# Down projection of a two-block model on one core: seven block products for 7 of 22 k pairs, and channel units in alternating pass order

## What is computed

```python
h = rmsnorm(x, g_ffn[l])                       # 256 x 2048
u = causal_dwconv(h @ w_up[l], ffn_conv_w[l]) + ffn_conv_b[l]
gate, val = jnp.split(u, 2, axis=-1)           # 256 x 5632 each
x = x + (jax.nn.silu(gate) * val) @ w_down[l]  # the down projection: 5632 x 2048 weights
...
return rmsnorm(x, g_final)
```

## Time and profile before

| | us |
|---|---|
| median of 3 runs | 1964.65 |
| lowest, highest | 1964.58, 1966.03 |
| the profiled execution | 1964.4 |
| its span, first to last instruction | 1962.6 |
| TensorE busy in it | 1944.7 (99%) |
| VectorE busy | 1289.4 (66%) |
| ScalarE busy | 1028.8 (52%) |
| granted TensorE clock | 0.999 of full |
| the down projection's matmuls | from 1713.8 to 1952.9, 239.1 |

### The profile page before, as it was taken

How to read it: one execution, slowest core, us unless ns; L and a number is a source line. 1 busy time by engine, 2 the same in 40 slices (tenths; PEclk the granted TensorE clock), 3 DMA queues, 4 the chain that set the end, 5 groups by cost and what they waited for, 6 DMA issues and landing times.

```text
span 1962.6 us, 28709 instructions
## 1 busy us (share of the span) xinstructions
PE 1944.7 (99%) x9868; PEld 1645.5 (84%) x9868; DVE 1289.4 (66%) x1806; ACT 1028.8 (52%) x1503; POOL 47.1 (2%) x74
## 2 busy tenths in 40 slices
PE   8999999999999999999999999999999999999998
PEld 7788888888888888888888888888888888888886
DVE  6655675656655676655768765778778787754444
ACT  5533576664433576654544444555555555544443
POOL 1000030000000020000100000000000000000000
PEclk9999999999999999999999999999999999999999
DMA  8666445545566545545666445556555565565553
GB/s 297 202 194 192 143 157 154 160 151 186 182 195 193 147 161 172 155 155 181 209 193 190 154 168 186 181 183 192 184 190 190 184 192 184 191 214 193 194 193 139
DMA packets 246726, 357.29 MB, mean 182 GB/s; under 512 B 15303, under 2 KB 136481, under 8 KB 246109
## 3 DMA queue, kind: packets, MB, share of 16 engines
q1 hardware_dynamic: 245004, 349.35, 55.8%
q0 software_dynamic: 1616, 6.61, 1.0%
HBM read 352.75 MB, written 3.16 MB: 181 GB/s over the span
## 4 chain that ended last, share of the span: by engine, by line
PE 96%; DVE 1%; ACT 1%; issue 1%; DMA 1%; SPq 0%; DVEq 0%; ACTq 0%
PE acc L368 21%; PE acc L345 19%; PE acc L347 19%; PE acc L346 19%; PE acc L361 11%; PE aux L425 2%; PE aux L833 1%; DVE sb_w_lo L308 1%; PE aux L851 1%; PE aux L850 1%; PE aux L814 1%; DMA sb_stage<-w_kv 0%; PE aux L820 0%; PE aux L822 0%; PE aux L821 0%
## 5 line engine op out<-in xcount | busy, mean ns | idle before, releaser
L308 DVE TENSOR_TENSOR sb_w_lo<-sb_stage,sb_w_hi 128x1024 fp32r<-128x1024 f32 x652 | 799.4, 1228 | 513.8 <-ACT sb_w_hi L303 506.9
L303 ACT ACTIVATE sb_w_hi<-sb_stage 128x1024 fp32r<-128x1024 f32 x652 | 688.7, 1059 | 640.4 <-PE acc L347 372.0
L368 PE MATMUL acc<-sb_xT,sb_w_hi 128*128 128x512 f32 x1856 | 455.3, 392 | 0.0
L368 PEld LDWEIGHTS acc<-sb_xT,sb_w_hi 128*128 128x128 f32 x1856 | 337.6, 189 | 62.6
L345 PE MATMUL acc<-sb_w_hi,sb_xT 128*128 128x512 f32 x768 | 306.6, 399 | 0.4 <-issue 0.4
L347 PE MATMUL acc<-sb_w_hi,sb_xT 128*128 128x512 f32 x768 | 299.8, 390 | 0.0
L346 PE MATMUL acc<-sb_w_lo,sb_xT 128*128 128x512 f32 x768 | 299.6, 390 | 0.0
L361 PEld LDWEIGHTS acc<-sb_xT,sb_w_lo 128*128 128x128 f32 x1856 | 245.6, 191 | 13.3
L361 PE MATMUL acc<-sb_xT,sb_w_lo 128*128 128x256 f32 x1856 | 252.3, 284 | 0.0
L345 PE MATMUL acc<-sb_w_hi,sb_mT 128*128 128x512 f32 x560 | 224.9, 402 | 1.6 <-issue 1.0
L347 PE MATMUL acc<-sb_w_hi,sb_mT 128*128 128x512 f32 x560 | 218.8, 391 | 0.0
(11 more groups left out here) (255 smaller groups left out, 1472.0 us busy)
## 6 DMA issues: line engine op xcount, KB each, us to landing
sb_stage<-w_in SPq DMA_DIRECT2D x248, 512.0 KB, 3.9
sb_stage<-w_up SPq DMA_DIRECT2D x176, 512.0 KB, 3.4
sb_stage<-w_out SPq DMA_DIRECT2D x96, 512.0 KB, 3.5
sb_stage<-w_down SPq DMA_DIRECT2D x88, 512.0 KB, 4.3
sb_stage<-w_kv SPq DMA_DIRECT2D x16, 512.0 KB, 6.8
sb_stage<-w_ukv SPq DMA_DIRECT2D x16, 512.0 KB, 3.4
sb_stage<-w_uq SPq DMA_DIRECT2D x12, 512.0 KB, 3.5
sb_kz<-mem SPq DMA_DIRECT2D x8, 256.0 KB, 7.2
```

The costliest lines, as they stand in the source:

```text
L303: act.activation(w_hi[:, j % RING, 0:size], stage[:, j % RING, 0:size], ACT.Copy).then_inc(hi_ready, 1)
L308: dve.tensor_tensor(w_lo[:, j % RING, 0:size], stage[:, j % RING, 0:size], w_hi[:, j % RING, 0:size].bitcast(F32), ALU.subtract).then_inc( ...
L368: mm = pe.matmul(acc[:, 2 * pair + c, :], hi[:, k, c * P:(c + 1) * P], both, start=first and k == 0, stop=last and k == 3)
```

## The change

It has two parts.

**Pass order.** In `product_cols` the unit at k tile 0 and the one at k tile 8 take the main passes first, the other two the rest passes first. Before, only the one at k tile 0 did. The table is a row of the TensorE program: one group of four units in the first turn of the feed-forward loop, before and then after (`sb_w_hi` is a main pass, `sb_w_lo` a rest pass).

The core of the diff:

```diff
+SEVEN = 7
+DOWN_PAIRS = [[[7, 8], 0, [9, 10], 1, [11, 12], 2, [13, 14], 3, [15, 16], 4, [17, 18], 5, [19], 6, [20, 21]],
+              [[7, 8], 0, [9, 10], 1, [11, 12], 2, [13, 14], 3, [15], 4, [16], 5, [17], 6, [18, 19, 20, 21]]]
...
+    for chunk, items in enumerate(DOWN_PAIRS):
+        for item in items:
+            if isinstance(item, list):
+                units += [("rows", k, 2 * chunk + half) for half in range(2) for k in item]
+            else:
+                units += [(f"seven{part}", item, chunk) for part in range(4)]
...
-            if first:
+            if (k0 // 4) % 2 == 0:
                 main_passes()
                 mm = rest_passes()
             else:
...
+        def round_down(act, j):
...
+            if kind != "seven2" and kind != "seven3":
+                act.wait_ge(staged[slot], 16 * (U4 // RING + down_loads(j)))
+            if kind == "seven1" or kind == "seven2":
+                act.wait_ge(sums_ready, 2 * sevens - 1)
+            if kind == "seven3":
+                act.wait_ge(sums_ready, 2 * sevens)
+                n = 512
+            act.wait_ge(unit_used, U4 + (j - RING + 1))
+            act.activation(w_hi[:, slot, 0:n], stage[:, slot, 0:n], ACT.Copy).then_inc(hi_ready, 1)
...
+            if kind == "seven0":
+                own, mixed, sums = (stage[:, (j + i) % RING, :] for i in range(3))
+                for i in range(2):
+                    dve.wait_ge(staged[(j + i) % RING], 16 * (U4 // RING + down_loads(j + i)))
+                dve.wait_ge(lo_ready, U4 + (j - 1))
+                step(dve.tensor_tensor(sums[:, 0:512], own[:, 0:512], mixed[:, 0:512], ALU.add))
+                step(dve.tensor_tensor(sums[:, 512:UNIT], sums[:, 0:512], own[:, 512:UNIT], ALU.add))
+                dve.tensor_tensor(mixed[:, 0:512], mixed[:, 0:512], own[:, 512:UNIT], ALU.add).then_inc(sums_ready, 1)
+                rest_unit(dve, U4, j)
...
+                    pe.wait_ge(lo_ready, U4 + (j + 1))
+                    passes(m_first, near(k, 0), 0, left, first, last)
+                    pe.wait_ge(lo_ready, U4 + (j + 2))
+                    passes(m_seventh, near(k, 1), 1, left, first, last)
+                    passes(acc[:, 2, :], mixed(2), 0, right).then_inc(unit_used, 1)
+                    passes(acc[:, 0, :], near(k + 1, 0), 1, right).then_inc(unit_used, 1)
+                    pe.wait_ge(lo_ready, U4 + (j + 3))
+                    passes(m_fifth, mixed(0), 2, left, first, last)
+                    passes(m_sixth, mixed(1), 2, right, first, last).then_inc(unit_used, 1)
+                    pe.wait_ge(lo_ready, U4 + (j + 4))
+                    passes(acc[:, 1, :], near(k + 1, 1), 3, left).then_inc(unit_used, 1)
...
+                    step(dve.tensor_tensor(first, a21, a22, ALU.subtract))
...
+                    step(dve.tensor_scalar(seven_T[:, pair, 0, :], mixed, 1.0, None, ALU.mult))
+                    dve.tensor_tensor(seven_T[:, pair, 1, :], mixed, seven_T[:, pair, 0, :].bitcast(F32), ALU.subtract)
...
+                    if j - 1 in SEVEN_END:
+                        add_sevens(SEVEN_END.index(j - 1), False)
+                    if j - 2 in SEVEN_END:
+                        add_sevens(SEVEN_END.index(j - 2), True)
+                    if j in DOWN_END[:3]:
+                        c = DOWN_END.index(j)
+                        add_to_x(dve, U4, j, c % 2, c)
...
-    nc = _bacc.Bacc("TRN2", target_bir_lowering=False, num_devices=1)
+    nc = _bacc.Bacc("TRN2", target_bir_lowering=False, num_devices=1, dynamic_dma_scratch_size=2048)
```

More of the change, by code:

```diff
@@ L115 @@
 DVE_STEPS_LAYER = 91
-FIRST_FFN_STEPS, FFN_STEPS = 15, 7
+FIRST_FFN_STEPS, FFN_STEPS, SEVEN_STEPS = 15, 7, 12
 X_SCORE = [41, 44, 47, 50]
@@ L648, in _ @@
                                  w_up2[:, 4 * i:4 * i + 4, bass.ds(turn_ * 256 + half * D_FF, 256)], 256)
-                for c in range(4):
-                    for i in range(FT // 2):
-                        load(sp, U4, (FT // 2) * c + i, w_down2[:, 2 * i:2 * i + 2, c * 512:(c + 1) * 512], 512)
+                for j, (kind, i, c) in enumerate(DOWN):
+                    if kind == "rows":
+                        load(sp, U4, j, w_down2[:, 2 * i:2 * i + 2, c * 512:(c + 1) * 512], 512)
+                    if kind == "seven0":
+                        load(sp, U4, j, crossed(2 * i, 2 * c, 1), 512)
+                    if kind == "seven1":
+                        load(sp, U4, j, crossed(2 * i, 2 * c + 1, -1), 512)
                 for t in range(T):
@@ L1111, in _, with product_seven, passes @@
                     ffn_turn(turn_)
[L1113 to L1118, removed]
+                def product_seven(j, i, first, last):
+                    k = 2 * i
+                    near = lambda k_, t: lambda h: act_T[:, k_, h, t * P:(t + 1) * P]
+                    mixed = lambda n: lambda h: seven_T[:, i, h, n * P:(n + 1) * P]
+                    def passes(o, a, part, cols, start=False, stop=False):
+                        slot = (j + part) % RING
+                        hi, lo = w_hi[:, slot, cols], w_lo[:, slot, cols]
+                        pe.matmul(o, a(0), hi, start=start, stop=False)
+                        pe.matmul(o, a(0), lo, start=False, stop=False)
+                        return pe.matmul(o, a(1), hi, start=False, stop=stop)
+                    left, right = slice(0, 512), slice(512, UNIT)
+                    pe.wait_ge(lo_ready, U4 + (j + 1))
[9 more added lines that the diff above has]
+                    passes(acc[:, 1, :], near(k + 1, 1), 3, left).then_inc(unit_used, 1)
@@ new lines, in _ @@
+                for j, (kind, i, c) in enumerate(DOWN[:DOWN_TAIL]):
+                    if c == 0:
+                        pe.wait_ge(act_ready, i + 1)
+                    if kind == "rows":
+                        first = j == 0 or all(unit[0] != "rows" or unit[2] != c for unit in DOWN[:j])
+                        if first:
+                            banks_free(pe, PAIRS4, c)
+                        product_rows(pe, U4, j, act_T, 2 * i, 2, 512, c % 2, first, j == DOWN_END[c])
+                    if kind == "seven0":
+                        if c == 1 and sevens_before(j) == SEVEN:
+                            pe.wait_ge(seven_free, 1)
+                        product_seven(j, i, sevens_before(j) % SEVEN == 0, j + 3 == SEVEN_END[c])
```

140 lines of the change are left out of this document (100 added, 40 removed).

## The result

The changed kernel takes 1994.3 us (median of four runs, 1989.4 to 1994.9) against 1964.8 before: 1.0144 times as long, 95% interval 1.0128 to 1.0159. I had forecast 1970.1 and a range of 1963 to 1979: right that it is slower, wrong in size: 24 us between the medians, 19 for the profiled execution, and above even the clearly slower case of the forecast (1975 to 1985).

What follows compares the result with a forecast made beforehand. TensorE was taken as the bound. Gains of 10.7 us (9.5 + 1.2) against losses of 16.2 added 5.5 to the profiled 1964.4, giving 1969.9, so a median of 1970.1 us; range 1963 to 1979.

Steps and rivals of the forecast that it cites:

- clearly slower case: Whole kernel: loads need 4.4 us throughout, so it takes 1975 to 1985 us; chance 0.16.
- Matmuls and pass order: On TensorE: 42 matmuls fewer gain 9.5 us, and 58 groups each gaining a join gain 1.2 us.
- The feed-forward additions: Feed-forward loop: six short VectorE instructions in 7 turns, 2.1 us a turn, cost nothing behind TensorE's own units.
- Two plain pairs between blocks: Down stage, eight stretches: load loop of 15.5 to 15.9 us against TensorE's 15.64 loses 0.1 each, 0.8 us in all.
- One plain pair: Down stage, four stretches: TensorE waits 1.0 and then 1.07 us in each, 8.1 us in all.
- The chunk boundary: Behind the first chunk pair's last block: TensorE waits 2.7 us for the accumulator pair, then loses 2.1 for seven1.
- The end: Behind the last block of all: the tail's waits of 1.3 and 0.8 us lose 2.1 together.
- Rival 2: Down stage: loads need 4.4 us throughout, 24.9 lost, 1978.9 us; its sign, TensorE waits at every block; chance 0.16.
- rival 1: Down stage: burst loads land sooner, 9.9 us lost against 10.7 gained, about even at 1963.8 us; chance 0.33.
- Rival V: Down stage, posed with the experiments: VectorE's added work itself sets the pace; no chance given.
- rival C: Down stage, posed with the experiments: TensorE's clock causes the loss; no chance given.

Runs made afterwards that it cites:

- E1: The kernel before with only the pass order of the change; 1963.38 us against 1964.47.
- E4: The changed kernel with the weight sums in a tile of their own and the ring counted by loads; 1965.9 us.
- E2: The changed kernel with each load of w_down 128 columns wide instead of 512; 1959.0 us.
- E3: The changed kernel with each of a block's four weight sums 32 columns wide instead of 512; 1968.7 us.
- E11: The changed kernel with five of 22 k pairs by seven products instead of seven, and three plain pairs between most blocks; 1966.8 us.
- E5: The kernel before with the down stage's loads started two at a time; 1965.9 us.
- E12: The changed kernel itself run again as a control; 1991.2 us, ratio 1.0133.
- E10: The changed kernel with each of the eight additions of the seven products to x 8 columns wide instead of 512; 1983.4 us.
- E6: The changed kernel with each seven-product block's two crossed loads replaced by plain loads of the same size; 1985.6 us.
- E7: E4 with the down stage's ring of loads eight slots long instead of four, the new ones under xT; 1963.0 us.
- E8: E7 with VectorE's work at the chunk boundary put in another order; 1961.0 us.

## Why the prediction was right or wrong

**Matmuls and pass order: right.** 42 matmuls went, at 0.2267 each. The pass order brings 1.1 us in E1 where I had 1.2.

**The feed-forward additions: right at nothing.** They take VectorE 2.0 us a turn where I had 2.1, and TensorE is as busy as before where they are made (177.07 of 178 us against 177.06).

**Two plain pairs between blocks: this step failed.** The loop was the right one, with the right links, and it was said to be at the edge (15.5 to 15.9 against 15.64). Two of its terms were mis-sized: the load close behind another, taken as 4.5, took 5.3; the next one, taken as 3.5 to 3.9, took 5.1 (and 5.5 and 4.3 a round later). That is 2.0 to 2.4 us more in the one round, 17.9, and 1.4 to 1.8 in the other, 17.3. A stretch loses 1.8 in the mean (1.1 to 2.5) instead of 0.1, eight 14.2 instead of 0.8. E4 and E2 show the cause, by taking time of the loads out of the loop in two ways. E3 and the first half of E11 fit its arithmetic; the second half of E11 loses more than it says. The wrong choice was to give the unfavourable burst rows to the one-pair stretches alone. Their second load needs 5.2; had I put that in place of 4.5, the loop would have come to 16.2 to 16.6 us, and the eight stretches to 5 to 8 us lost. In the two-pair stretches the four remainders of a block come bunched too, so their loads start at gaps of 1.7, 1.1 and 0.6 us, and the fifth comes behind three that are still under way. Why a load in such company needs 5.1 to 5.5 us rather than the 4.9 of E5's pairs, no run takes apart. A loop that I had put within 0.1 us of TensorE's time needed the bunching in every one of its loads, and my far end for it, 6 us, still had a lone load of 4.4.

**One plain pair: mechanism right, size at its far end.** 2.9 us a stretch in the mean, which is the 2.9 worked out for loads of 0.9 more; I took 2.0. Seven1's load, the fourth of the burst, needs 6.1 to 6.7 us there, not 5.4. E12 shows it cleanly, with 2.8 to 3.2 a stretch. In the profiled execution the same 11.5 for the four is partly an accident: they lose 1.7 to 4.5 each, and 1.6 of it is a stretch at half clock.

**The chunk boundary: mechanism right, sum partly by accident.** The wait for the acc pair took 2.6 us against 2.7 forecast (3.5 in E12), for the reason given: E10, where VectorE's additions are narrow, has no such wait. But the additions need the late loads beside them: in E4 and E2, which keep all additions, the wait for the acc pair is 0.3 us. In the profiled run the second part, 2.1 for seven1, was smaller (0.4), but 1.7 at half clock and 0.9 in front of the second plain unit came in, which I hadn't forecast, so that the sum, 5.7 against 4.8, isn't much of a test. E12 has 1.8 for seven1 and no half clock, and E4 and E2, with the loads in time, have 1.8 too, so that term stands.

**The end: 2.9 against 2.1.** The two waits forecast, 1.3 and 0.8 in the tail, measure 1.4 and 0.7. A third of 0.7, in front of the second plain unit behind the last block, wasn't forecast. That unit's load is again the close one that I took as 4.5, and a wait of up to 1.0 us stands at the same place in most stretches. E4 removes the end's loss wholly, so it too hung on a load.

**The rivals.** Rival 2 had the direction: loads slow everywhere, 24.9 us lost. It gave the loads 4.4 where they took 5.3, and so it was short by 10, with a chance of 0.16 that was too small; the time lies beyond even its range. Its sign, that TensorE waits at nearly every block, did show. In rival 1 the fourth load of the burst was put at 0.8 after the block by the figures given there; 1.2 us for each further load make it 1.4. Both are far from what came: with the 6.3 us of the burst shown above it lands at 3.8. Rival V and rival C are out as main causes: E4 keeps VectorE's work, and E12 loses 35.9 us without one stretch at half clock.

**Open:** how much of the loads' time is the crossed pattern (E6, one run), why the loads of a burst need as long as they do, why E11's second chunk pair still waits, and why the changed kernel's other three runs in its first set lie 5 us above the profiled one; with them a fifth of the miss between the medians has no trace.

## What to carry to other kernels

Where instructions are taken from the engine that bounds a kernel, draw the loop through the buffer ring afresh. A scheme that holds a ring's slots for something other than loads, or frees them in bunches, makes loads start late and together, and the latency to put into such a loop is that of a burst (5.1 to 5.5 us here), not that of an even stream (3.5 to 4.4). Give derived data (sums) a buffer of its own and count the ring by loads; and check at the first use of new slots from when they are free.

## What the hardware did that I had not expected

Four loads of 512 KB issued at gaps of 1.7, 1.1 and 0.6 us need 3.4, 5.5, 5.6 and 6.3 us. Two issued 0.41 us apart need 4.1 and 4.9. Of eight issued within 5.4 us at E7's start, the first needs 5.8 and the last 10.2.

TensorE's granted clock drops to 0.50, the 1.2 GHz level, where the matmuls stand 0.427 us apart and not 0.2267, in or right behind waits of 2.1 to 3.5 us in all. In the changed kernel it does so twice, for 3.4 us each, once behind a wait of 2.6 us and once behind 1.2 and 0.9 in short order. In E10 it is 3.4 us behind 1.6 and 0.9. At the start of E7 and E8, with waits of 0.7 or 0.8 and then 2.7, it is 6.8 and 3.4 us. In E6, with a wait of 3.1 us for the acc pair, it is 6.8 us. Each time that costs 1.5 to 2.8 us on top of the waits. Yet in E12 TensorE waited 3.5 us in E6's place, and elsewhere 1.3 and 0.9 in short order, and stayed at the full level. So the drop doesn't follow from the length of the waits alone, and what decides it is open.
